# MLA heads 0 to 14: three of four probability tiles turned by VectorE blocks and DRAM, gating moved behind the keys

## The reference

```python
h = x @ w_in
c_q, c_kv, k_rope, g = jnp.split(h, ...)
q = (_rms_norm(c_q, q_norm) @ w_q_up)        # 16 heads of 128 + 64 (rope)
kv = (_rms_norm(c_kv, kv_norm) @ w_kv_up)    # 16 heads of 128 keys + 128 values
p = softmax(where(mask, (q_nope k_nope + q_rope k_rope) * scale, neg))
o = p @ v
return (o * silu(g)) @ w_out
```

## Time and profile before

| | us |
|---|---|
| median of three runs (2168.88 to 2171.07) | 2170.91 |
| the profiled execution, its own time | 2170.27 |
| its span in the profile | 2168.5 |
| DVE, ACT, POOL busy in the span | 1284.7, 836.7, 1175.3 |

### The profile page before, as it was taken

One profiled execution on the slowest core, in us unless ns is written; L12 is line 12 of the kernel. 1 busy time (PEld: TensorE's weight loads), 2 busy tenths in 40 slices (PEclk: granted clock), 3 DMA queues, 4 the chain that ended last, 5 costly groups with the idle time before them and its releaser, 6 DMA issues.

```text
span 2168.5 us, 50089 instructions
## 1 busy us (share of the span) xinstructions
PE 2141.5 (99%) x20795; PEld 1715.8 (79%) x20795; DVE 1284.7 (59%) x2558; ACT 836.7 (39%) x1726; POOL 1175.3 (54%) x829
## 2 busy tenths in 40 slices
PE   8999999999999999999999999999999999999999
PEld 6888887788888767777777777777779788888877
DVE  5465467877850666666666666666652476656621
ACT  4122212333320354555555555555432444444410
POOL 5555566688766264544555544544566453443455
PEclk9999999999999999999999999999999999999999
DMA  4322323333332143333333333333534322222132
GB/s 131 88 78 78 88 88 91 94 97 97 97 110 96 42 126 87 83 82 83 82 92 83 88 87 91 88 90 92 145 79 126 107 78 54 67 56 54 54 129 95
DMA packets 368490, 193.77 MB, mean 89 GB/s; under 512 B 124411, under 2 KB 348793, under 8 KB 367881
## 3 DMA queue, kind: packets, MB, share of 16 engines
q1 hardware_dynamic: 368074, 190.50, 31.8%
q10 hardware_dynamic: 191, 0.07, 0.0%
HBM read 159.18 MB, written 18.52 MB: 82 GB/s over the span
## 4 chain that ended last, share of the span: by engine, by line
PE 93%; DVE 3%; POOL 1%; ACT 1%; issue 1%; DMA 0%; SPq 0%; DVEq 0%; POOLq 0%; ACTq 0%
PE ps L1452 21%; PE ps L161 16%; PE ps L162 15%; PE ps L163 15%; PE ps L1691 4%; PE ps L1707 3%; PE ps L1566 2%; PE ps L1737 2%; PE ps L1680 2%; PE ps L2791 2%; PE ps L1606 1%; PE ps L1651 1%; PE ps L1599 1%; PE ps L1638 1%; PE ps L2775 1%
## 5 line engine op out<-in xcount | busy, mean ns | idle before, releaser
L152 POOL TENSOR_TENSOR w_lo<-raw,w_hi 128x1024 fp32r<-128x1024 f32 (+1 forms) x163 | 416.1, 2553 | 13.6
L149 POOL TENSOR_SCALAR w_hi<-raw 128x1024 fp32r<-128x1024 f32 (+1 forms) x163 | 182.3, 1118 | 399.6 <-PE ps L163 383.2
L161 PE MATMUL ps<-h_hi,w_hi 128*128 128x512 f32 x616 | 242.9, 394 | 2.9 <-DVE h_lo L1129 1.7
L162 PE MATMUL ps<-h_lo,w_hi 128*128 128x512 f32 x616 | 240.8, 391 | 0.0
L163 PE MATMUL ps<-h_hi,w_lo 128*128 128x512 f32 x616 | 240.7, 391 | 0.0
L1452 PE MATMUL ps<-mixed_k,raw 128*64 128x264 f32 x1024 | 146.6, 387 | 0.0
L1452 PE MATMUL ps<-mixed_r,raw 128*64 128x264 f32 x1024 | 144.0, 387 | 0.2 <-ACT ws_b L1771 0.2
L161 PEld LDWEIGHTS ps<-h_hi,w_hi 128*128 128x128 f32 x616 | 116.1, 188 | 28.7 <-DVE h_lo L1129 2.6
L1452 PE MATMUL ps<-mixed_g,raw 128*64 128x264 f32 x1024 | 137.6, 387 | 0.0
L163 PEld LDWEIGHTS ps<-h_hi,w_lo 128*128 128x128 f32 x616 | 116.1, 189 | 24.4
L162 PEld LDWEIGHTS ps<-h_lo,w_hi 128*128 128x128 f32 x616 | 116.2, 189 | 23.1
(11 more groups left out here) (499 smaller groups left out, 5793.4 us busy)
## 6 DMA issues: line engine op xcount, KB each, us to landing
raw<-in_rwkv_w_in_dram SPq DMA_DIRECT2D x64, 512.0 KB, 4.4
raw<-in_w_up_dram SPq DMA_DIRECT2D x44, 512.0 KB, 3.9
raw<-in_w_in_dram SPq DMA_DIRECT2D x41, 512.0 KB, 3.9
raw<-in_w_down_dram SPq DMA_DIRECT2D x22, 512.0 KB, 3.5
raw<-in_mla_w_in_dram SPq DMA_DIRECT2D x22, 512.0 KB, 4.0
sb_kept<-xT SPq DMA_DIRECT2D x16, 528.0 KB, 2.6
xT<-sb_kept SPq DMA_DIRECT2D x16, 528.0 KB, 3.8
raw<-in_mla_w_out_dram SPq DMA_DIRECT2D x16, 512.0 KB, 3.6
```

Source lines behind the costliest of these rows:

```text
L149: nc.gpsimd.tensor_scalar(w_hi[s][:, 0:width], raw[s][:, 0:width], 1.0, 0.0, ALU.mult, ALU.add).then_inc(split_hi, 1)
L152: nc.gpsimd.tensor_tensor(w_lo[s][:, 0:width], raw[s][:, 0:width], w_hi[s][:, 0:width].bitcast(F32), ALU.subtract).then_inc(split_ready, 1)
L161: nc.tensor.matmul(dst, w[0], x[0], start=start, stop=False)
L162: nc.tensor.matmul(dst, w[0], x[1], start=False, stop=False)
```

## The change

For heads 0 to 14, tiles 0, 1 and 2 are no longer turned on PE. DVE transposes each tile in 32x32 blocks within SBUF (`blocked`: one instruction for the tile, one for the strip with the spilled keys, into `wa_in` and a new buffer `p_third`), SP writes the blocks to DRAM in four DMAs per tile in runs of 32 numbers (`write_blocks`), so that they lie transposed as a whole, and reads the tile back into `probT` in one DMA (`read_turned`): 12 writes and 3 reads per head. The strips are copied by DVE from SBUF to SBUF (`spilled`). Tile 3 is still turned on PE. Head 15 stays as it was.

With it go: `values` of the head before is moved behind score tile 2; `kb` and `v2` are filled into PSUM bank 2; `gated` and the three `spilled` copies come behind `low_out(kb)`; on POOL `z_low` comes behind the split of the next 1280-column unit; the loads of units are issued by SP in the gaps of the new DMAs. The semaphores are three of the first block's, used again.

```diff
@@ -2433,6 +2433,11 @@
         assert put.end <= 121
         probT, z_t = xT[:, 0:5, 0:T1], xT[:, 7, 0:T1]
         prob = xT[:, 5:7, :].rearrange("p a b -> p (a b)")
+        p_scr = [[nc.dram_tensor(f"p_scr{t}_{e}", [P * (t + 1), P], F32, kind="Internal").ap() for t in range(QB - 1)] for e in range(2)]
+        p_third = region(154)("p_third", [P, T1])
+        p_blocked, p_written, p_here = x_land[0:3]
+        LANDED0 = 16
+        BLOCKED, WRITTEN, HERE = 3, 192, 48
...
-        BANK_OF = {"v0": 4, "v1": 5, "v2": 4, "rope": 4, "gate": 6, "ka": 5, "qn": 4, "kb": 5}
+        BANK_OF = {"v0": 4, "v1": 5, "v2": 2, "rope": 4, "gate": 6, "ka": 5, "qn": 4, "kb": 2}
...
@@ -2757,20 +2762,64 @@
             slot = T2 * (1 - t % 2)
             return prob[:, slot + at:slot + at + n]
 
+        def blocks_of(t):
+
+            return (wa_in[:, 0:P], wa_in[:, P:3 * P], p_third[:, 0:3 * P])[t]
+
+        def spill_of(t):
+
+            return p_third[0:32, 3 * P + 32 * t:3 * P + 32 * t + 32]
+
+        def write_blocks(sp, h, t):
+            sp.wait_ge(p_blocked, LANDED0 + BLOCKED * h + t + 1)
+            if t == 0 and h > 1:
+                ge(sp, p_here, LANDED0 + HERE * (h - 1))
+            for a in range(4):
+                sp.dma_start(p_scr[h % 2][t].rearrange("(b i) q -> i b q", i=32)[:, :, 32 * a:32 * a + 32],
+                             blocks_of(t)[32 * a:32 * a + 32, :].rearrange("i (b j) -> i b j", j=32)).then_inc(p_written, 16)
+
+        def read_turned(sp, h, t):
+            q = slice(P * t, P * t + P)
+            sp.dma_start(probT[:, 0:t + 1, q], p_scr[h % 2][t].rearrange("(c p) q -> p c q", p=P)).then_inc(p_here, 16)
+
+        def turned_by_dma(sp, h, loads):
+
+            written = LANDED0 + WRITTEN * h
+            write_blocks(sp, h, 0)
+            write_blocks(sp, h, 1)
+            next(loads, None)
+            sp.wait_ge(p_written, written + 128)
+            ge(sp, oo_mm, h)
+            read_turned(sp, h, 0)
+            read_turned(sp, h, 1)
+            write_blocks(sp, h, 2)
+            sp.wait_ge(p_written, written + WRITTEN)
+            read_turned(sp, h, 2)
+            next(loads, None)
+
+        def unit_loads(sp):
+            for unit in MLA_UNITS:
+                load_mla(sp, unit)
+                yield
+            for k in range(3):
+                load_out_rows(sp, k)
+                yield
+
         def turn_bank(t):
             return 2 + t % 2
 
         def spill_cols(h, t):
 
-            at = P * min(t + 1, QB - 1)
-            return (turn_bank(t) if t < QB - 1 else value_bank(0) if h < MH - 1 else 2), at
+            return 2 + (t % 2 if t < QB - 1 else 0), P * min(t + 1, QB - 1)
 
         def turn(pe, h, t):
             pe.wait_ge(sc_norm, 4 * h + t + 1)
-            if h or t >= 2:
-                pe.wait_ge(pt_ev, 4 * h + (0, 0, 1, 2 if h < MH - 1 else 3)[t])
-            if h and t == QB - 1:
+            if t >= 2 and h == MH - 1:
+                pe.wait_ge(pt_ev, 4 * h + (1, 3)[t - 2])
+            if t == QB - 1 and h == MH - 1:
                 pe.wait_ge(zt_ev, h)
+            elif t == QB - 1:
+                pe.wait_ge(fill_dve, DVE_AFTER[FILL_AT["kb", h + 1]])
             for c in range(t + 1):
                 nc.tensor.transpose(ps[:, turn_bank(t), P * c:P * c + P], prob_cols(t, P * c, P), ident[:])
             bank, at = spill_cols(h, t)
@@ -2782,6 +2831,8 @@
         def values(pe, h):
 
             e, bank = h % 2, value_bank(h)
+            if h < MH - 1:
+                pe.wait_ge(p_here, LANDED0 + HERE * (h + 1))
             pe.wait_ge(pt_ev, 4 * h + 4)
             pe.wait_ge(fill_act, ACT_AFTER[FILL_AT["v2", h // 2]])
             if h:
@@ -2835,11 +2886,13 @@
             scores(pe, h, 1)
             between(0)
             first_out(pe, h, 0)
-            if h:
+            if h == MH - 1:
                 values(pe, h - 1)
-            turn(pe, h, 0)
-            turn(pe, h, 1)
+                turn(pe, h, 0)
+                turn(pe, h, 1)
             scores(pe, h, 2)
+            if 0 < h < MH - 1:
+                values(pe, h - 1)
             between(1)
             if h == MH - 2:
                 fill(pe, FILL_AT["gate", MH - 1], range(5, KD))
@@ -2850,7 +2903,8 @@
             if h + AHEAD < MH:
                 fill(pe, FILL_AT["gate", h + AHEAD], range(2, 5) if h == MH - 3 else range(4, KD))
             first_out(pe, h, 3)
-            turn(pe, h, 2)
+            if h == MH - 1:
+                turn(pe, h, 2)
             turn(pe, h, 3)
 
         def out_pe(pe):
@@ -2888,8 +2942,13 @@
             slots = items_of(h)
             for t in range(QB):
                 act.wait_ge(sc_max, 4 * h + t + 1)
-                if h or t >= 2:
-                    act.wait_ge(pt_mm, 4 * h + max(t - 1, 0))
+                if t >= 2 and h == MH - 1:
+                    act.wait_ge(pt_mm, h + t - 1)
+                elif t >= 2:
+                    act.wait_ge(p_blocked, LANDED0 + BLOCKED * h + t - 1)
+                elif h:
+                    act.wait_ge(p_blocked, LANDED0 + BLOCKED * h)
+                    act.wait_ge(pt_mm, h)
                 dst = prob_cols(t, 0, keys(t))
                 if t == QB - 1:
                     dst = dst.rearrange("p (a b) -> p a b", a=2)
@@ -2944,28 +3003,44 @@
                 nc.vector.tensor_scalar(p, p, prec[:, t % 2:t % 2 + 1], None, ALU.mult).then_inc(sc_norm, 1)
 
             def turned_out(t):
-                dve.wait_ge(pt_mm, 4 * h + t + 1)
-                if h:
-                    dve.wait_ge(oo_mm, h)
+                dve.wait_ge(pt_mm, h + 1 + (t if h == MH - 1 else 0))
+                dve.wait_ge(oo_mm, h)
                 bank, at = spill_cols(h, t)
                 nc.vector.tensor_copy(probT[0:N_META, t + 1, P * t + P - 32:P * t + P], ps[0:N_META, bank, at + P - 32:at + P])
                 nc.vector.tensor_copy(probT[:, 0:t + 1, P * t:P * t + P],
                                       ps[:, turn_bank(t), 0:P * (t + 1)].rearrange("p (a b) -> p a b", b=P)).then_inc(pt_ev, 1)
-            turns = h % 2 == 1 and h < MH - 1
+
+            def blocked(t):
+                dve.wait_ge(sc_norm, 4 * h + t + 1)
+                if t == 0:
+                    ge(dve, p_written, LANDED0 + WRITTEN * h)
+                    ge(dve, pt_ev, 4 * h)
+                nc.vector.transpose(blocks_of(t), prob_cols(t, 0, P * (t + 1)))
+                slot = T2 * (1 - t % 2) + P * (t + 1)
+                nc.vector.transpose(spill_of(t), prob[96:P, slot:slot + 32]).then_inc(p_blocked, 1)
+
+            def spilled(t):
+                dve.wait_ge(p_blocked, LANDED0 + BLOCKED * h + t + 1)
+                ge(dve, oo_mm, h)
+                nc.vector.tensor_copy(probT[0:N_META, t + 1, P * t + P - 32:P * t + P], spill_of(t)[0:N_META, :]).then_inc(pt_ev, 1)
+            last = h == MH - 1
+            turns = h % 2 == 1 and not last
             maximum(0)
             maximum(1)
             normalise(0)
             normalise(1)
             if not turns and h < MH - 1:
                 rope_parts(dve, h + 1)
-            if h:
+            if last:
                 gated(dve, h - 1)
-            turned_out(0)
-            turned_out(1)
+            for t in range(2):
+                turned_out(t) if last else blocked(t)
             maximum(2)
             if turns:
                 rope_turned(dve, h // 2 + 1)
             normalise(2)
+            if not last:
+                blocked(2)
             if h == MH - 2:
                 gate_out(dve, MH - 1)
             maximum(3)
@@ -2975,9 +3050,15 @@
             if h + 1 < MH:
                 for kind in ("ka", "qn", "kb"):
                     low_out(dve, (kind, h + 1))
+            if not last:
+                if h:
+                    gated(dve, h - 1)
+                for t in range(QB - 1):
+                    spilled(t)
             if h + AHEAD < MH - 1:
                 gate_out(dve, h + AHEAD)
-            turned_out(2)
+            if last:
+                turned_out(2)
             turned_out(3)
 
         def z_low(pool, h):
@@ -3010,11 +3091,13 @@
                 sp.dma_start(h_rows_kept, h_rows[:]).then_inc(s_h, 16)
                 for n in range(4, 7):
                     load_in(sp, n)
-                for unit in MLA_UNITS:
-                    load_mla(sp, unit)
-                for k in range(2):
-                    load_out_rows(sp, k)
-                load_out_rows(sp, 2)
+                loads = unit_loads(sp)
+                for _ in itertools.islice(loads, 6):
+                    pass
+                for h in range(MH - 1):
+                    turned_by_dma(sp, h, loads)
+                for _ in loads:
+                    pass
                 sp.wait_ge(unit_done, UNIT_AT["gate", MH - 1] + 1)
                 sp.wait_ge(s_h, 48)
                 sp.dma_start(h_fin[:], h_rows_kept).then_inc(s_h, 16)
@@ -3045,10 +3128,10 @@
                 for h in range(MH - 1):
```

(6 more changed lines are left out.)

## The result

The changed kernel takes 2187.43 us (median of four runs, 2187.28 to 2188.1) where the kernel before takes 2170.14 on the same chip: a ratio of 1.0081, 95% interval 1.0063 to 1.0098. It is slower, by 17 us; 12 were forecast. The profiled execution took 2187.28 us, its span is 2185.6 against 2168.5 before.

The account below looks back on a forecast made before the run. PE was taken to bound the kernel, with 93% of the chain. Heads +4.7 and the end of head 14 +7.3 gave +12.0 on 2170.27, forecast 2182 us; range 2168 to 2192, the forecast's own 2176 to 2187.

Parts of the forecast that it names:

- The removed transposes: PE, per head: 0.50 + 0.43 = 0.93 us of transposes taken away, 14 us over 15 heads if all shows.
- The split: POOL's w_lo ends at W (start of its 1280-column w_hi) + 4.29; PE's fill waits, returning about 0.34 of 0.43 us.
- The port: DVE and POOL share SBUF: cast or copies held until w_lo ends, maximum(0) at W + 6.1, 1.7 us late.
- Odd and even heads: Odd heads 21.1 us against 19.98, score tile 3 waiting for exponential 2; even heads 20.2 against 20.54, PE last.
- rival 2: Small copies pass beside POOL, cast wins the port; odd heads PE-bound at 19.4 us; 2170.6 us, 2166 to 2175; chance 0.14.
- The end of head 14: POOL's output split comes behind z_low(13); PE stands about 7.8 us, +7.3 net; head 14 up to its kb -0.5.
- Transfers: Last read of tile 2 issued at W + 25.3, landed 27.5, wanted 28.6; 0 to 7 us possible, nothing taken.
- rival 1: As the forecast, plus a late transfer or the last small copy losing the port to z_low; 2186 to 2199 us; chance 0.17.

Follow-up runs that it names:

- run 7: Kernel of run 3 with only gated made early, behind blocked(2), the spilled copies still behind low_out(kb): 2162.8 us, ratio 0.9964.
- run 6: Kernel of run 3 with only the three spilled copies made early, behind blocked(2), gated still behind low_out(kb): 2164.49 us, ratio 0.997.
- run 3: Changed kernel with both edits at the end of head 14, those of run 1 and run 2 together: 2172.99 us, ratio 1.0015.
- run 9: Kernel of run 3 with the two groups swapped, the three spilled copies first, then gated: 2171.79 us, ratio 1.0008.
- run 4: Changed kernel with gated and the spilled copies made early, behind blocked(2) and not behind low_out(kb): 2168.51 us, ratio 0.9997.
- run 5: Changed kernel with the edits of run 3 and run 4 together: 2167.68 us, ratio 0.9988.
- run 1: Changed kernel with POOL making z_low(13) behind the split of the first output unit, not ahead of it: 2177.78 us, ratio 1.0039.
- run 2: Changed kernel with SP, in head 14, loading the third output rows behind the reads of the turned tiles: 2182.22 us, ratio 1.0057.

## Why the forecast was right, and where it was short

- **The removed transposes are worth having.** Where the port costs PE nothing, a pair of heads takes 19.24 + 20.07 = 39.31 us (run 7) against 40.55 before, 0.62 us per head of the 0.93 removed. What the prediction's terms leave is 0.93 - 0.34 = 0.59.
- **The split**: the term was right. In head 10, after W at 1961.94, PE is through with score tile 1 and due at about W + 4.05, as forecast (its last product starts at 1965.86, and the next would follow by 0.12), and the fill starts when `w_lo` has ended, at W + 4.33 (4.39 forecast):

```profile
1965.86 0.29 PE L2758 MATMUL ps<-kr_lo,qr 128*128 128x272 f32 x1
1966.27 0.39 PE L161 MATMUL ps<-w_hi,ckv_hi 128*128 128x256 f32 x1
```

  Where the cast has won the port, `w_lo` ends 0.2 us later and PE starts at W + 4.5 to 4.6. The forecast took this case, W + 4.64, for even heads, and there it is the exception: head 2 takes 20.21 us (20.2 forecast), and so do the even heads of run 6, 20.22, but ahead of heads 4 to 12 the cast loses. So even heads gain 0.51 us and not 0.34. In run 6 the late `w_lo` costs odd heads 0.22 us against run 7.
- **The port**: right in place, size and outcome. Cast due at W + 1.32, found between W + 1.27 and W + 1.42; `maximum(0)` at W + 6.1, found at W + 5.91 to 6.04. The 16x32 copy, bounded by 0.1 and 2.6 us with the upper end taken, stands for 2.91 us. Runs 3, 6, 7 and 9 show the cause. What I missed is in head 1: without a cast ahead, the copies are due at W + 0.57 and pass. Forecast 21.1 or up to 1.5 less, found 19.29. The Trainium skill, "SBUF — State Buffer", Who interferes with whom, says that issue order and not the op's shape decides who is blocked; runs 6, 7 and 9 agree, a copy of 16 partitions standing 2.9 us and one of the same kind passing in 0.16 us.
- **Odd and even heads**: 21.1 and 20.2 forecast, 21.02 and 20.05 found. The rival's 19.4 for odd heads without the port (rival 2) is found in runs 4 to 7, 19.2 to 19.5.
- **Head 13**: 22.55 us, 1.5 more than the other odd heads. It waits 2.68 us on exponential 2, since only two chunks of the last gate stand in its way, and then has 3.4 us at half clock. In runs 3 and 9 the same wait, 2.65 and 2.75 us, passed without it, and head 13 took 21.02 and 20.84. So the 1.5 us are the clock.
- **The end of head 14 is the step that failed**, by size: -0.5 + 7.3 = +6.8 forecast, +15.3 found (all behind W of head 13). The wait itself was forecast as 7.8 us and is 7.70. Missing were the 3.42 us wait on the read of tile 2 and 2.1 + 2.8 us at half clock, together 8.3 us. Of the moved loads the prediction said that one has 15 us to spare; it had asked for whom the load waits, and not who stands behind it in SP's queue when that wait is long. The mechanism was on the table: POOL's late split was forecast, and `load_out_rows` waits for it.
- **Transfers**: the read of tile 2 was put at W + 25.3 and 1 us in time. It is issued at W + 21 (1942.05 for head 8, after W at 1920.92). About half of the difference is that a write takes SP 0.46 us and not 0.65. Taking nothing for it was right, the reason given was too tight. The penalty below 512 B that the prediction cites from the Trainium skill ("DMA: Bandwidth & Descriptors", Specifications) can't be told apart here: such writes land in 1.5 to 2.3 us (medians of the three sizes), and no run writes the same blocks in longer pieces.

The misses of +8.5 at the end, -1.7 in heads 1 to 13, and -1.7 ahead of them (2.2 us found, 0.5 forecast) make the 5 us between 12 and 17. Part of the closeness is luck. In heads 1 to 13 the 1.5 us of clock in head 13, forecast nowhere, make up for most of the 1.8 us that head 1 was put too high, and the miss ahead of the heads is mostly outside the change. The 2187.43 us lie just outside the forecast's own 2176 to 2187 and inside the numbers of rival 1, but its mechanism was not found: no transfer comes late before head 14, where the cause is SP's load, and no copy loses the port to `z_low`.

## What to carry to other kernels

When an instruction is moved, list every queue that it or its successors pass, and for each wait on such a queue ask what is issued behind it: a load that "has time" can hold a read that hasn't. A copy or cast of DVE from SBUF to SBUF, however small (16x32 here), has a due time against POOL's long instructions; count to the tenth of a microsecond, and put what has no haste where POOL is idle. Two groups that are each free can cost together, so test a move of two in all four combinations.

## What was not expected of the hardware

- Three copies of 16x32 elements, held while `w_hi` ran, went through between it and `w_lo` (the third from W + 1.29 to 1.46, 0.06 us before and 0.11 after `w_lo` began), and one due at W + 1.48 stood 2.91 us (run 7).
- A PE wait of 2.65 to 2.68 us in head 13 was followed by 3.4 us at 1.2 GHz in the changed kernel and in runs 1 and 2, and by none in run 3, with the same code up to there; one of 2.75 us in run 9 by none. In head 14 a wait of 1.78 us went with 3.4 us of it (run 7), those of 1.71 (run 6) and 2.89 us (run 1) with none, those of 7.70, 3.42 and 4.24 us (run 5) with 6.8 us each.
- 128x128 and 128x256 transposes of DVE between SBUF tiles take 0.31 and 0.45 us beside a running `w_lo`, where a copy of 16x32 is held for 2.91 us.
